# Forming the low parts of streamed weights by whole chunks instead of by halves

## The reference, cut to what matters

```python
def swiglu(h, w_in, w_out):
    gate, up = jnp.split(h @ w_in, 2, axis=-1)
    return (jax.nn.silu(gate) * up) @ w_out        # 1024 -> 2 x 2816 -> 1024

for layer in range(DEPTH):
    shift, scale, gate = jnp.split((c @ mod_w[layer, 0] + mod_b[layer, 0])[:, None, :], 3, axis=-1)
    h = rms_norm(x, norm_w[layer, 0, 0]) * (1.0 + scale) + shift
    y = mixer(h)
    x = x + gate * rms_norm(y, norm_w[layer, 0, 1])
    ...                                            # the same around swiglu
```

## Time and profile before

| | us |
|---|---|
| median of 3 runs | 1466.71 (1466.6 to 1468.67) |
| the profiled execution | 1464.96 |
| its span | 1463.1 |
| PE busy | 1267.9 (87%) |
| DVE busy | 1016.3 (69%) |
| ACT busy | 593.3 (41%) |
| DVE, forming LO (340 instructions) | 410.7 |
| ACT, forming HI (340 instructions) | 338.8 |

### The profile page before, as it was taken

One profiled execution on the slowest core, in us unless ns is written; L12 is line 12 of the kernel. 1 busy time (PEld: TensorE's weight loads), 2 busy tenths in 40 slices (PEclk: granted clock), 3 DMA queues, 4 the chain that ended last, 5 costly groups with the idle time before them and its releaser, 6 DMA issues.

```text
span 1463.1 us, 22569 instructions
## 1 busy us (share of the span) xinstructions
PE 1267.9 (87%) x9684; PEld 1185.3 (81%) x9684; DVE 1016.3 (69%) x1578; ACT 593.3 (41%) x965; POOL 183.7 (13%) x199
## 2 busy tenths in 40 slices
PE   2897879999998977879999956999999858999997
PEld 0785558899997965869999936999988627999997
DVE  5746565878866567587876598676668995755554
ACT  1432354444444433554343523444453106544443
POOL 0000001000001000033900073000005660000000
PEclk9897779999999988989999977999999979999999
DMA  9851304477773652527677503787733202355540
GB/s 384 308 201 62 140 30 173 167 282 299 266 265 133 220 213 92 211 84 288 247 282 290 209 39 131 272 310 284 271 145 116 87 29 88 136 213 225 191 157 30
DMA packets 39301, 276.78 MB, mean 189 GB/s; under 512 B 4368, under 2 KB 4896, under 8 KB 6304
## 3 DMA queue, kind: packets, MB, share of 16 engines
q1 hardware_dynamic: 36864, 268.45, 49.1%
q0 software_dynamic: 1040, 3.70, 0.7%
q10 hardware_dynamic: 1296, 3.18, 0.6%
HBM read 273.72 MB, written 1.07 MB: 188 GB/s over the span
## 4 chain that ended last, share of the span: by engine, by line
PE 69%; DVE 23%; ACT 4%; DMA 1%; issue 1%; POOL 0%; ACTq 0%; SPq 0%; DVEq 0%
PE PS L357 68%; DVE raw L1161 4%; DVE LO L1171 4%; DVE TMP L1209 2%; DVE HLo L1204 1%; DMA raw<-WS 1%; DVE SQ L1534 1%; ACT HI L820 1%; DVE SC L1308 1%; ACT RS L820 1%; DVE SC L1297 1%; DVE TMP L1235 1%; ACT HH L820 1%; DVE SC L1322 1%; DVE SQ L1535 1%
## 5 line engine op out<-in xcount | busy, mean ns | idle before, releaser
L357 PE MATMUL PS<-HH,HI 128*128 128x256 f32 x1952 | 564.5, 289 | 52.8 <-ACT HH L820 30.4
L357 PE MATMUL PS<-HLo,HI 128*128 128x256 f32 x1952 | 565.5, 290 | 22.0 <-DVE HLo L1204 21.6
L357 PE MATMUL PS<-HH,LO 128*128 128x256 f32 x1952 | 560.0, 287 | 0.0
L1171 DVE TENSOR_TENSOR LO<-raw,HI 128x1024 fp32r<-128x1024 f32 x340 | 410.7, 1246 | 155.5 <-ACT HI L820 155.5
L357 PEld LDWEIGHTS PS<-HH,HI 128*128 128x128 f32 x1952 | 382.8, 196 | 61.3 <-ACT HH L820 33.9
L357 PEld LDWEIGHTS PS<-HLo,HI 128*128 128x128 f32 x1952 | 381.4, 195 | 27.1 <-DVE HLo L1204 25.6
L357 PEld LDWEIGHTS PS<-HH,LO 128*128 128x128 f32 x1952 | 382.6, 196 | 0.5 <-issue 0.5
L820 ACT ACTIVATE HI<-raw 128x1024 fp32r<-128x1024 f32 x340 | 338.8, 1048 | 107.6 <-PE PS L357 101.6
L1161 DVE CUSTOM_DVE_ANT_0 raw<-raw,CB,SM 128x1024 f32<-128x1024 f32 x168 | 212.4, 1296 | 12.8 <-DMA SM<-small 11.2
L357 PE MATMUL PS<-HDH,LO 128*128 128x256 f32 x704 | 199.2, 283 | 0.0
L357 PE MATMUL PS<-HDL,HI 128*128 128x256 f32 x704 | 198.8, 282 | 0.0
(11 more groups left out here) (189 smaller groups left out, 1169.1 us busy)
## 6 DMA issues: line engine op xcount, KB each, us to landing
raw<-WS SPq DMA_DIRECT2D x255, 1024.0 KB, 5.1
SC<-scratch POOLq DMA_DIRECT2D x2, 1024.0 KB, 9.6
X<-xT ACTq DMA_DIRECT2D x1, 1024.0 KB, 14.4
SC<-ssm POOLq DMA_DIRECT2D x2, 512.0 KB, 4.8
out<-TMP SPq DMA_DIRECT2D x1, 1024.0 KB, 3.9
CB<-vecs ACTq DMA_DIRECT2D x1, 512.0 KB, 7.0
SC<-SC ACTq DMA_DIRECT2D x4, 128.0 KB, 8.0
CB<-vecs POOLq DMA_DIRECT2D x1, 512.0 KB, 5.7
```

The source lines that it names most:

```text
L357: return e.matmul(o, l, r, start=start, stop=stop, skip_group_check=True)
L1171: e.tensor_tensor(LO[:, s % HL, :], raw_half(j, h), HI[:, s % HL, :].bitcast(fp32), O.subtract).then_inc(*D.up(("lo", s)))
```

## The change

The two subtractions of a chunk become one over all its 2048 columns. It is emitted where the second half is handed out; nothing is emitted for the first half. Its event marks both units. Since unit numbers of a chunk are even and odd, the six slots serve as three pairs of neighbours. The bookkeeping changes with it: a first half is handed out only when both units that used the pair before are done with, and a second half then needs no slot of its own. `high` stays as it is: two instructions of 1024 columns.

```diff
@@ -149,8 +149,8 @@
         a = self.unit
         while self.unit < min(n + 1 + ahead, len(self.units)):
             j, h = self.units[self.unit]
-            s = self.order.get((j, h))
-            if j >= self.load or (s is not None and s >= HL and s - HL not in self.hl):
+            s = self.order.get((j, 1)) if h == 0 else None
+            if j >= self.load or (s is not None and s >= HL and not {s - HL - 1, s - HL} <= self.hl):
                 assert self.unit > n
                 break
             if h == 1:
@@ -1167,9 +1167,12 @@
                         gemv(j, plan[j][1], h)
                     elif plan[j][0] == "w":
                         s = order[j, h]
-                        w.wait_ge(*A.at(("hi", s)))
-                        e.tensor_tensor(LO[:, s % HL, :], raw_half(j, h), HI[:, s % HL, :].bitcast(fp32),
-                                        O.subtract).then_inc(*D.up(("lo", s)))
+                        if h == 1:
+                            i = s % HL - 1
+                            w.wait_ge(*A.at(("hi", s)))
+                            e.tensor_tensor(flat(LO[:, i:i + 2, :]), rawt[:, j % RAW, :],
+                                            flat(HI[:, i:i + 2, :]).bitcast(fp32), O.subtract) \
+                                .then_inc(*D.up(("lo", s - 1), ("lo", s)))
```

## The result

The changed kernel takes 1572.74 us (median of 4 runs, 1571.11 to 1577.95); the kernel before, on the same chip, 1466.81 (1466.6 to 1468.67). The ratio is 1.0729, with a 95% interval of 1.0714 to 1.0745: 7.3% slower. The forecast was 1555, the range 1518 to 1585. The profiled execution took 1571.11 us with a span of 1569.2, so the span grew by 106.1.

The account below looks back on a forecast made before the run. The prediction took PE to bound the feed-forward stages (264 of 340 halves), with DVE having time to spare. Terms 45 + 8.4 + 8.4 + 8 + 20 = 90 us on 1464.96 gave 1555 us, range 1518 to 1585.

Parts of the forecast that it names:

- The rival "faster": Whole kernel: pairs in time everywhere and 12 us of DVE come off the chain, 1453 us; chance 3%.
- Part 1: Low parts on DVE: 170 instructions replace 340, each pair taking 2.28 us, saving about 0.07 us a pair.
- Part 2: Odd in-chunks of f0 to f3, 21 places: PE stops 2.05 us each, 4.0 at f1 j = 9; 45 us.
- part 7: Clock falls behind 30 stops of 2 to 4 us: half of them at 1.3 us, 20 us (0 to 39).
- Part 3: j = 5 and 19 of f0, f1, f2, where PE already waits: 6 x 1.4 = 8.4 us.
- Part 4: Start of a stage, j = 3 of f0, f1, f2: 3 x 2.8 = 8.4 us.
- Part 6: Stricter slot rule, high parts of first halves and raw slots later: costs nothing, at most 1.06 us at three places.
- Part 5: Stages outside the feed-forward ones (abo, cdo, ab, in2, cd, glu, o2) and tails of f0, f1: 8 us (6 to 10).
- a part of 1.5: Tails of f0 and f1 and the pairs of glu and o2: some 1.5 us together.
- the clock falls behind nearly each: Rival for the whole kernel: stops come and the clock falls behind nearly each, 1574 us; chance 12%.

Follow-up runs that it names:

- Experiments 2: Changed kernel with each pair's low part formed by two 1024-column instructions, both standing where the wide one stands: 1514.72 us, ratio 1.0323.
- experiments 3: Changed kernel, wide instructions kept, with the planner's look-ahead rounded up so a weight chunk's second half is handed out with its first: 1499.47 us, ratio 1.0209.
- 5: Kernel before, its 340 narrow instructions kept, with the look-ahead rounded up so second halves are handed out with first halves: 1465.25 us, ratio 0.9984.
- experiment 9: Rounded-up look-ahead, one wide instruction only for the 96 pairs expected early, two narrow ones elsewhere: 1469.64 us against 1469.57 for the kernel before, ratio 0.9996.
- experiment 1: Kernel before with only the slot rule changed: a first half waits until both slots of its pair are free: 1467.66 us against 1467.31, ratio 1.0006.
- experiment 4: Changed kernel with matmuls on zeros put on TensorE ahead of the 30 feed-forward waits for low parts: 1539.53 us, ratio 1.0488.
- experiment 8: Changed kernel with pairs formed by one instruction only in stage f2, two narrow instructions everywhere else: 1499.0 us, ratio 1.0198.
- experiment 7: Changed kernel with pairs formed by one instruction only outside the four feed-forward stages, narrow instructions inside them: 1480.11 us, ratio 1.0087.

## Why the prediction was right

**Direction and mechanism.** The forecast said that the time at which a low part is ready counts and not its cost. Experiments 2, 3 and 5 show it: with narrow instructions and the rounded-up look-ahead 1465 us, with wide ones 1499, with narrow ones at the second half's place 1515, with wide ones there 1573. And VectorE's time saved shows nowhere (in experiment 9 LO takes 398 us of it in place of 411, and the kernel's time is that of before). Of the two rules of the Trainium skill (Perfetto Trace Analysis, Optimizing Scalar/DVE Operations) the one on breaking instructions up where an unsaturated engine holds up another gives the sign here, 1.0729. The rival "faster" (DVE's time comes off the chain) fell: DVE's share of the chain rose from 23 to 27%.

**Part 1**, 2.28 us: 2.29 where GpSimd rests, 2.304 in the mean.

**Part 2**, 2.05 us at 21 places: 17 of them measured 2.04 to 2.12. Two errors within it. At f1's j = 11 PE had already stopped for 2.07 us, in the same chain; after, it is 2.06, and the change added nothing there. I had counted that stop as new in this part and as evidence in part 7 without putting the two together. And f1's j = 9 came out at 3.76 for 4.0, but not by a low part of 3.4 us. DVE, ACT and PE there, after:

```profile
766.87 2.06 DVE L1161 CUSTOM_DVE_ANT_0 raw<-raw,CB,SM 128x1024 f32<-128x1024 f32 x1
...
768.86 0.41 DVE L1276 TENSOR_TENSOR HF<-SIL,PS 128x256 f32<-128x256 f32 x1
...
769.31 0.42 ACT L820 ACTIVATE HDH<-HF 128x256 fp32r<-128x256 f32 x1 [2.21 <-DVE HF L1276]
...
770.70 2.29 DVE L1173 TENSOR_TENSOR LO<-raw,HI 128x2048 fp32r<-128x2048 f32 x1 [0.35 <-ACT HI L820]
...
773.05 0.38 PE L357 MATMUL PS<-HH,HI 128*128 128x256 f32 x1 [3.50 <-DVE LO L1173]
```

The pair itself takes 2.29; the gemvs ahead of HF take 2.06 each, in GpSimd's stretch, and HF comes late. The right size for a wrong reason: luck. The last three (f0's j = 9 and 11, f1's j = 7) have 0.2 to 1.3 us more than 2.05, which makes up by chance for the 2.05 counted at j = 11: 44.5 us net for 45.

**Part 3**, 8.4: 8.7 (stops of 2.98 to 3.54 where 1.57 to 2.14 stood). **Part 4**, 8.4: 7.2; f1 and f2 2.76 and 2.77, f0 less, since PE had stopped there already, twice, for 0.97 and 0.94. Parts 2 to 4 together 60.4 for 61.8.

**Part 6**, nothing: for the slot rule shown by experiment 1. The raw slots, freed later, cost nothing either: in the kernel after the high parts wait 2.8 us for DMA in the whole run, 2.9 before.

**Part 7, the clock: mis-sized.** 20 us, 15 falls at 1.3. The traces have 19 falls of 30, at 1.48 (two at 2.24), less the 1.5 of in11.0 in f1: 28 us; experiment 4, which takes the falls away and leaves the stops, gives 32 for the whole kernel. Both factors were low. The price was misread: the window of 3.40 us behind 737.45 holds the whole slow stretch, but its count of 18 takes in two matmuls that were running at its start, and the 28 that it was set against takes in none. A window of the same length at a clock of 1.00, also of the kernel before, has 30, so 12 are lost and not 10:

```profile
941.00:944.40 3.40, 3.40 (x30) 3.40 (x30) 0.55 (x2) 0.48 (x2) 0.00 (x0) 1.00 0.91 301
```

12 x 0.12 = 1.44 us, and 4.37 us is what the first half of in11.0 took already there. And one of two was too thin a sample for the chance. That the term needed wide ends is seen in experiment 8: 12.4 us in a stage that had 8.8 in the kernel after.

**Part 5, the other stages: mis-sized.** 8 us; 14.4 between the traces, 12 alone (experiment 7). The places were right and single prices were near: abo, where PE started at 218.44, starts at

```profile
223.26 0.55 PE L357 MATMUL PS<-HH,HI 128*128 128x256 f32 x1 [6.90 <-DVE LO L1173]
```

4.8 us later, 2.4 of them carried over from ab and 0.4 from the attention in between; its wait for LO grew from 4.90 to 6.90, 2.0 for 1.9. What I had not thought of is the clock here too. Between f0 and cd PE does only the sums of the norm and matmuls on zeros, which the kernel has there before and after. The windows from f0's last product to cd's first, of the kernel before and then of the kernel after, each with lines of PE and ACT from there (in the second also DVE's low parts that lie across its start):

```profile
456.72:472.65 15.93, 11.49 (x86) 9.16 (x84) 11.32 (x27) 6.14 (x17) 3.92 (x5) 1.00 0.21 89
...
466.33 0.70 PE L357 MATMUL PS<-SQ,means 128*128 128x256 f32 x2 [3.17 <-POOL SQ L1630]
...
469.24 0.47 ACT L820 ACTIVATE RS<-PS,eps 128x256 f32<-128x256 f32 x1 [1.36 <-PE PS L357]
```

```profile
492.54:511.71 19.17, 14.39 (x86) 10.97 (x84) 12.08 (x31) 6.13 (x17) 3.92 (x5) 0.82 0.24 100
...
488.15 4.49 DVE L1173 TENSOR_TENSOR LO<-raw,HI 128x2048 fp32r<-128x2048 f32 x2 [1.47 <-ACT HI L820]
...
493.24 1.99 PE L357 MATMUL PS<-SQ,means 128*128 128x256 f32 x8 [0.53 <-DVE SQ L1228]
...
502.78 1.22 PE L357 MATMUL PS<-SQ,means 128*128 128x256 f32 x2 [3.18 <-POOL SQ L1633]
...
508.30 0.47 ACT L820 ACTIVATE RS<-PS,eps 128x256 f32<-128x256 f32 x1 [3.98 <-PE PS L357]
```

The same 86 matmuls take 3.25 us longer. Up to the second group of sums (466.33 and 502.78) it is 0.6: there the first sums wait for DVE, which forms two wide LO until 492.64. From it to ACT's next step it is 5.52 us in place of 2.91, 2.6 more, with the granted clock averaging 0.82 over the window where it was 1.00. I had a part of 1.5 for the whole, so the 0.6 was in it and the 2.6 was not. The fall is no fixed price of the change: in experiments 3 and 7 the same step is 0.6 longer than before and in experiment 4 2.2, and before the change PE stopped there for 3.17 us too, with the clock staying up. It was not tried alone.

**The total.** 106 us against 90: 60.4 + 28 + 14.4 + 3. The miss of 16 us is 8 from the clock and 10 outside the feed-forward stages and in small steps, less 1 from the stops. The rival "the clock falls behind nearly each" came nearer in number, 1574, but not in fact: 19 of 30 fell, and its missing 11 us of clock are made up, by chance, by the 10 us that were not foreseen outside the feed-forward stages and in small steps.

## What to carry to other kernels

Before joining two instructions into one, look up for each consumer which of the two it waits for, and how much slack it has: joining moves the readiness of the first to the end of the second, and costs the wait for the second's input and the length of the second instruction, here 2 us times 30 for 14 us of engine time saved. Where the slack was over 2 us (the 96 pairs of experiment 9) joining cost PE 0.6 us of waits, and as the engine was not the bound it brought nothing either. And count a stop of TensorE between busy stretches with what may follow it: here half as much again as the stops themselves.

## What the runs showed of the hardware

- Behind stops of TensorE of the same length the granted clock fell to 0.50 in some cases and not in others: of 17 stops of 2.04 to 2.12 us in the kernel after 11, of its 13 longer ones 8. In the same stage with the same stops it was six of nine in one kernel and eight of nine in another. What decides it in a single case these runs don't show.
- Behind short stops no unit was slow. Counted over the ten traces without added matmuls (that of the kernel before among them), ahead of the in-chunks from j = 3 on: none of 72 stops of 0.37 to 1.93 us had a slow unit behind it, 21 of 31 stops of 2.04 to 2.20 us had one, and 22 of 29 longer ones. Many of them are the same place in several traces.
- A fall cost 1.48 us of 24 matmuls' time (4.36 for 2.88; twice it was 2.24), and with matmuls on zeros in the stops none came behind any of the 30: some 32 us for work whose result nobody reads.
- The 2048-column subtraction takes 2.29 us where two of 1024 in a row take 2.36 (both in the traces above): joining two of them brings 0.07 us. Beside GpSimd's work in f1 single ones took up to 2.90 us, and the multiply-and-sum of a "mod" half 2.06 in place of 1.28.
